# Feed-forward units of a transformer layer: VectorE splits the next unit's weights before it adds up the blocks of the one after

## The reference, cut to what matters

```
def swiglu(h, w_gu, w_down):
    gu = jnp.einsum('bsd,df->bsf', h, w_gu)
    gate, up = gu[..., :D_FF], gu[..., D_FF:]
    return jnp.einsum('bsf,fd->bsd', jax.nn.silu(gate) * up, w_down)

x = x + forgetting_attention(rmsnorm(x, mix_norm_g), ...)
x = x + swiglu(rmsnorm(x, ffn_norm_g), w_gu, w_down)
```

## Time and profile before

| | us |
|---|---|
| median of 3 runs | 2247.16 |
| lowest and highest run | 2244.59, 2248.47 |
| the profiled execution | 2246.37 |
| its span, first to last instruction | 2244.7 |
| TensorE busy | 2155.1 |
| VectorE busy | 1520.2 |
| ScalarE busy | 911.7 |

### The profile page before, as it was taken

How to read it: one execution, slowest core, us unless ns; L and a number is a source line. 1 busy time by engine, 2 the same in 40 slices (tenths; PEclk the granted TensorE clock), 3 DMA queues, 4 the chain that set the end, 5 groups by cost and what they waited for, 6 DMA issues and landing times.

```text
span 2244.7 us, 27898 instructions
## 1 busy us (share of the span) xinstructions
PE 2155.1 (96%) x10404; PEld 1864.5 (83%) x10404; DVE 1520.2 (68%) x2092; ACT 911.7 (41%) x1203; POOL 181.8 (8%) x356
## 2 busy tenths in 40 slices
PE   8999999999999999999999999999998989999997
PEld 8999999999998877877777787787787767777786
DVE  4444444444463447798897797797787786887778
ACT  5433333333343344445444444444344433333332
POOL 0322222122220000000000000000000010000000
PEclk9999999999999999999999999999999999999999
DMA  6332332333253345667666756756759869859855
GB/s 176 86 94 75 93 89 80 88 89 93 75 182 108 99 128 175 212 202 236 224 207 229 232 190 234 233 193 230 235 188 359 316 220 322 300 178 315 277 177 182
DMA packets 267132, 416.68 MB, mean 186 GB/s; under 512 B 16114, under 2 KB 114452, under 8 KB 266020
## 3 DMA queue, kind: packets, MB, share of 16 engines
q1 hardware_dynamic: 260496, 375.08, 51.9%
q10 hardware_dynamic: 6548, 40.40, 4.8%
HBM read 366.63 MB, written 48.79 MB: 185 GB/s over the span
## 4 chain that ended last, share of the span: by engine, by line
PE 70%; DVE 15%; DMA 12%; issue 1%; SPq 1%; ACT 0%; DVEq 0%; ACTq 0%
PE gemm L513 11%; PE gemm L515 11%; PE gemm L514 11%; DVE f_lo L1350 6%; PE gemm L714 6%; PE gemm L715 6%; PE gemm L716 6%; DMA f_raw<-in_ffn_w_gate_up 6%; PE aux L714 5%; PE aux L716 4%; PE aux L715 4%; DMA f_raw<-in_ffn_w_down 4%; DVE f_raw L1356 3%; DMA forms_scratch<-fa_b_lo 2%; DVE f_raw L1361 1%
## 5 line engine op out<-in xcount | busy, mean ns | idle before, releaser
L1350 DVE TENSOR_TENSOR f_lo<-f_raw,f_hi 128x2048 fp32r<-128x2048 f32 (+1 forms) x264 | 532.7, 2024 | 52.8 <-ACT f_hi L998 33.5
L513 PE MATMUL gemm<-w_hi,act_t 128*128 128x384 f32 (+2 forms) x1280 | 451.6, 353 | 3.0 <-DVE w_lo L1129 3.0
L514 PE MATMUL gemm<-w_lo,act_t 128*128 128x384 f32 (+2 forms) x1280 | 444.7, 347 | 0.0
L515 PE MATMUL gemm<-w_hi,act_t 128*128 128x384 f32 (+2 forms) x1280 | 444.6, 347 | 0.0
L714 PE MATMUL gemm<-f_hi,a_form 128*128 128x512 f32 x1056 | 418.8, 397 | 4.6 <-DVE rows L1431 3.1
L715 PE MATMUL gemm<-f_lo,a_form 128*128 128x512 f32 x1056 | 417.0, 395 | 0.0
L716 PE MATMUL gemm<-f_hi,a_form 128*128 128x512 f32 x1056 | 416.1, 394 | 0.0
L714 PE MATMUL aux<-f_hi,a_form 128*128 128x512 f32 x792 | 322.7, 407 | 70.3 <-DVE f_lo L1350 69.0
L716 PE MATMUL aux<-f_hi,a_form 128*128 128x512 f32 x792 | 313.8, 396 | 0.0
L715 PE MATMUL aux<-f_lo,a_form 128*128 128x512 f32 x792 | 313.6, 396 | 0.0
L1129 DVE TENSOR_TENSOR w_lo<-w_raw,w_hi 128x768 fp32r<-128x768 f32 (+1 forms) x160 | 160.7, 1008 | 208.5 <-ACT w_hi L809 208.5
(11 more groups left out here) (163 smaller groups left out, 2113.4 us busy)
## 6 DMA issues: line engine op xcount, KB each, us to landing
f_raw<-in_ffn_w_gate_up SPq DMA_DIRECT2D x264, 512.0 KB, 4.6
f_raw<-in_ffn_w_down SPq DMA_DIRECT2D x132, 512.0 KB, 5.3
w_raw<-in_fox_w_in SPq DMA_DIRECT2D x192, 256.0 KB, 3.3
f_raw<-in_ffn_w_gate_up SPq DMA_DIRECT2D x88, 256.0 KB, 4.1
a_form<-forms_scratch SPq DMA_DIRECT2D x22, 1024.0 KB, 9.0
forms_scratch<-hs_hi ACTq DMA_DIRECT2D x22, 896.0 KB, 5.1
a_form<-forms_scratch SPq DMA_DIRECT2D x22, 768.0 KB, 8.7
w_raw<-in_fox_w_out SPq DMA_DIRECT2D x16, 1024.0 KB, 5.1
```

The lines of the kernel that those rows point to most:

```text
L513: mm(out, a_hi, b_hi, start=first, stop=False)
L514: mm(out, a_hi, b_lo, start=False, stop=False)
L515: return mm(out, a_lo, b_hi, start=False, stop=last)
L1350: v.tensor_tensor(f_lo[:, n % 4, 0:3 + g], f_raw[:, n % 4, 0:3 + g], f32(f_hi[:, n % 3, 0:3 + g]), ALU.subtract).then_inc(f_lo_done, 1)
```

## The change

In iteration n of VectorE's loop, `weights_lo(n + 1)` now comes first, and `sums_t1_t3(n + 2)` after it, directly before `sums_t2_t4(n + 2)`. Iterations in which unit n + 2 is of the first pass have no block sums and stay as they are. The streams of TensorE, ScalarE and SyncE are the same.

```
                 sums = n + 2 < NU and UNITS[n + 2][1] == 1
-                if sums:
-                    sums_t1_t3(n + 2)
                 if n + 1 < NU:
                     weights_lo(n + 1)
                 if sums:
+                    sums_t1_t3(n + 2)
                     sums_t2_t4(n + 2)
```

## The result

The changed kernel takes **2269.43 us** (median of 4 runs, 2268.11 to 2272.66) against 2245.88 us for the kernel before on the same chip (4 runs, 2243.4 to 2248.47). The ratio is 1.0107, with a 95% interval of 1.0089 to 1.0124. The change makes the kernel slower by 1.1%. The forecast was 2288 with a range of 2268 to 2314. Sign and range held, the range by 1.4 us at its lower end, and the loss is little more than half of the 41.5 us of the sum: the profiled span is 2268.5 us against 2244.7, so 23.8 us longer.

A forecast was written before the change was run, and what follows sets the result against it. The prediction took the feed-forward as TensorE-bound except where VectorE's split comes late. Losses of 32.5 us (gate and up) and 9 us (down) made 41.5; 2247.2 + 41 = 2288 us, range 2268 to 2314.

The forecast's parts named there:

- the 41.5 us of the sum: Predicted loss over the whole kernel: 32.5 us in eleven gate-and-up rounds plus 9 us in six down rounds.
- F7's wait goes, S0 comes at L + 6.12: In round 6, F7's split no longer waits behind S0's load, and S0 starts on TensorE 2.66 us earlier.
- L: Moment S0's load lands and VectorE's line 1356 for S0 starts, 1370.71 in round 6; taken as unmoved by the change.
- The loop of 5.99 us: Second pass: split, block sums, ScalarE's rest and next split form a closed VectorE-ScalarE loop, period 5.99 against TensorE's 5.44 us.
- S1 at L + 13.53, S7 at L + 49.47: Round 6 matmul starts: S1 keeps 0.7 us of the gain; six more periods of 5.99 make S7 1.83 us late.
- The store, F1 2.95 us late: Gate-and-up rounds: the low part's store, issued 2.95 us later and taking 6.59, delays VectorE's reads and F1 by 2.95.
- The rival without the store's part: Store adds nothing, so a gate-and-up round loses 1.83 us; 29 us with the down rounds, total 2276; chance 0.16.
- The down rounds, 6 x 1.5: Six down rounds lose about 1.5 us each, 9 us together; less where more was lost at the step between passes.
- The clock: TensorE at 1.2 GHz costs nothing in S0 or S1; rival: 1.75 us behind F1 in ten rounds, 2305, chance 0.15.
- the rival with the clock lost all through: Many small waits lower TensorE's clock in every S unit, 7.2 against 5.99 us, adding 160: 2445; chance 0.03.
- the rival of 2276: Store adds no delay: 1.83 us lost per gate-and-up round, 9 in the down rounds, 29 us altogether; chance 0.16.

The follow-up runs named there:

- the split in halves: Changed kernel with each S unit's split as two 1024-column instructions, the first needing only the high part's first half: 2193.23 us, ratio 0.9762.
- the store's experiment: Against the kernel with the new order only at F7, the hidden state's second low-part store is issued ahead of S7's high part: 2227.52 us.
- start on the first half: Against the split in halves, TensorE starts S units on half the split, ScalarE reads products before S1's high part, hidden_hi(r, 1) moves to j 7: 2173.85 us.
- the longer loop: Changed kernel with ScalarE making an S unit's whole high part, 2048 columns, in one instruction behind line 1363: 2362.79 us, ratio 1.0525.

## Why the prediction was right, and where its sum was wrong

- **F7's wait goes, S0 comes at L + 6.12: right.** F7 has no wait, and S0 starts at L + 6.16 in round 6 (1385.28 to 1391.44), at L + 6.15 in the other gate-and-up rounds.
- **The loop of 5.99 us: right.** Measured 6.01; VectorE idles for 1.13 us before the split, as read off the end of the pass in the earlier trace rows, where the changed kernel's order stood already. One link longer by 0.86 lengthened the period by 0.92, and the split in halves brought 5.44 back.
- **S1 at L + 13.53, S7 at L + 49.47: right.** Measured L + 13.66 and, in round 6, L + 49.7 (1435.00, five periods behind S2 at 1404.95). The forecast left out a wait within S0: TensorE waits there 1.10 us for ScalarE's read, line 1018, since ScalarE's queue has the first half of S1's high part ahead of that read, and it waits for line 1356, which now stands behind S0's split. It costs nothing here, for S1 has to wait for the loop anyway.
- **The store, F1 2.95 us late: wrong.** This is the step that failed. I moved the store's landing by as much as its issue, with the 6.59 us of the earlier trace rows kept as if the duration belonged to the transfer. In the changed kernel it is 3.8 us at the median (6.5 before), VectorE waits for it twice and not ten times, and in round 6 it lands at L + 50.0, where the kernel before has L + 49.7: later by 0.3 us and not by 2.95. F1 comes at L + 59.41 where 60.45 stood in the sum, 1.91 us late, less than the 2.5 that the prediction named as the sign of this step being wrong. Of S7's lateness of about 2 us that is all that reaches F1, and nothing is added: the eleven rounds of gate and up lose 3.11, 2.44, 2.82, 3.77, 2.07, 1.90, 2.02, 1.33, 1.83, 1.69 and 0.42 us, together 23.4 and not 32.5. The rival without the store's part had 1.83 a round, and the rounds average 2.13. That rival also held that the store may land faster, and I gave it 0.16.
- **The down rounds, 6 x 1.5: mis-sized.** They change by -1.06, -1.81, +1.55, -0.13, +1.34 and +1.84 us, together 1.7 and not 9. The three near 1.5 are as worked out. In the other three the kernel before had lost more at the step between the passes: rounds 11, 12 and 14, with waits of 3.70, 3.48 and 3.05 us at the last F unit and a fallen clock behind them. The text named that ("will lose less") and gave it no number, though its rows could be read round by round.
- **The clock: right that it costs nothing in S0, and it did not fall behind F1.** F1 starts right behind F0. In front of S1 TensorE waits for 0.36 us in round 6 and not for 2, since 1.10 of it lie within S0. The mean granted clock is 0.987, where the kernel before has 0.982. The swing that the Trainium skill describes ("TensorE: Matmul & The Clock Gate", section A second HAM failure mode: psum-queue depth-cycling) did not come with 114 waits of 0.6 us in the mean. The price of the rival with the clock lost all through has a slip: 2288 and 160 make 2448, not 2445.

With -1.3 us ahead of the feed-forward, which the change does not touch, the parts make the span's difference: 23.4 + 1.7 - 1.3 = 23.8. The main reason, the loop, is shown. Of the forecast's surplus 9.1 us lie in the rounds of gate and up, the store's step, and 7.3 in the down rounds; the measured time is nearest to the rival of 2276, and the range held only because it reached down to 2268.

## What to carry to other kernels

Before moving an instruction ahead of a wait, ask what the instruction it passes was doing there: the block sum that looked like an obstacle in front of the split was also the work that filled VectorE while ScalarE made what the split needs. Sum each loop through two engines along every branch, and compare it with the pace of the engine that binds; where it is too long, cut an instruction in halves so that its first half depends on less, and each engine works while the other does. An order may be right at one place of a loop and wrong at the rest: try them apart, and read a wait by its count as well as by its total.

## What the hardware showed

- **The same store lands in 3.8 or in 6.5 us, later the closer it stands behind a load.** In the changed kernel the two loads that SyncE's queue issues ahead of it go out at 1428.78 and 1429.20, and the store of 896 KB 2.4 us behind the second, at 1431.56. Before, they went out at 1413.10 and 1413.52 and the store 0.3 us behind them, at 1413.81. The medians of the other traces fall in line: 0.8 us behind the load it takes 5.6 (the split in halves), 1.1 us behind it 5.2 (the store's experiment, which moved nothing else), 1.3 us behind it 4.8 (start on the first half), and 3.4 us behind it 3.6 (the longer loop). So up to 2.4 us of distance it lands, at the median, 6.1 to 6.8 us behind the load's issue, whenever it is issued itself. In these traces its landing followed the load's issue, which waits for TensorE, and not its own, which waits for ScalarE. No run took the load away, and in round 10 it takes 7 to 11 us in every trace, which this does not explain.

```profile
1428.78 0.38 SPq L366 DMA_DIRECT2D f_raw<-in_ffn_w_gate_up  x1
...
1431.56 0.33 ACTq L1066 DMA_DIRECT2D forms_scratch<-fa_b_lo  x1
```

- **TensorE's granted clock fell behind some waits and not behind others.** It fell behind 2.40 us in the kernel before and behind 2.05 with the new order at F7 alone (0.76), and stayed at 1.00 behind 1.59 in round 6 of the changed kernel, and in every S unit behind it with its wait of 0.2 to 0.4. But with the new order at F7 alone it also stayed up behind 2.87 us in round 1, and fell behind 1.84 in round 3; in the changed kernel it stayed up behind 2.06 in round 4 and fell behind 1.89 in round 7. So the length of the wait alone does not decide, and what does stays open.
